# Chunk attention two heads at a time, on alternating halves of the TensorE array

## The chip, the cores and the metric

The kernel runs on one core of a Trainium2 chip. The metric is the device time of one execution in microseconds: the median of 3 runs is 1926.85 us.

## What is computed

A two-layer streaming encoder over 512 frames of width 1024, in float32: an S5 and gated-DeltaNet mixer, memory cross-attention and a SwiGLU FFN in the first layer; chunk attention, cross-attention and FFN in the second. The change touches chunk attention alone (16 heads of 64, chunks of 64 frames, each attending to its own chunk and the 8 before it, which is here all that went before):

```python
q = rms_norm(qkv[:, :, 0], q_g); k = rms_norm(qkv[:, :, 1], k_g); v = qkv[:, :, 2]
def one_chunk(c):
    ...
    s = jnp.einsum('bqhd,bkhd->bhqk', q_c, k_c) * scale + bias
    s = jnp.where((band_pos + start) >= 0, s, -1e30)
    p = jax.nn.softmax(s, axis=-1)
    return jnp.einsum('bhqk,bkhd->bqhd', p, v_c)
```

## The kernel before, in words

Each engine has its own instruction stream, written out by hand; semaphores (`wait_ge`, `then_inc`) tie them together, and the order of a stream is the order of the calls in it. `ca_pe`, `ca_act`, `ca_dve` and `ca_sp` are the parts of chunk attention on TensorE, ScalarE, VectorE and the SP queue.

Queries and keys stand transposed in SBUF, `cqT` and `ckT`: head h occupies partitions 64*(h % 2) to 64*(h % 2)+63 of plane h // 2, so a product of them uses half of the array's rows. The 512 queries of a head are four blocks i of 128; block i sees the keys 0 to 128*(i+1), so its scores are 128*(i+1) wide. One head goes through:

- scores, TensorE (`ca_scores_pe`, L1761): four products into PSUM banks 0 to 3. A float32 product of this kind stands in the trace as two passes, each with its own weight load.
- sums, VectorE (`ca_dve.sums`, L1838 to L1848): a mask of 64x64 on the bias, then `tensor_tensor_reduce` (L1844) adds the bias, writes the block to SBUF (`p_c`) and takes each row's maximum. In the trace this is CUSTOM_DVE_ANT_0 with a read-out of the accumulator.
- exponentials, ScalarE (`ca_act.exps`, L1821), in place, with row sums.
- rescale, VectorE (L1859, L1862): reciprocal, then four multiplies in place.
- transposes, TensorE (`ca_turn_p_pe`, L1771): ten blocks of 128x128, in four groups s of 4, 3, 2 and 1 into PSUM banks 4 to 6 in turn.
- copies (`ca_copy`): group s goes to SBUF (`pT_c`), 0 and 3 by ScalarE (L1793), 1 and 2 by VectorE (L1795).
- values, TensorE (`ca_values_pe`, L1780): four products of 128 rows with 64 columns of weights, into partitions 0 to 63 or 64 to 127 of bank 7.
- output, in two parts that sum to float32: ScalarE copies bank 7 to `c_oT[0]` (L1831), rounded; VectorE subtracts that from bank 7 into `c_oT[1]` (L1853, `out_lo`).

TensorE's order is transposes of h, scores of h+2, values of h. `p_c` and `pT_c` have two sets each. The bias of each head comes by a DMA on SP's queue into a ring of four. GpSimd has nothing to do in this stage. After it the output projection begins (`split_outproj_pe`, L308 to L310). Before it, query and key rows are transposed (`ca_turn_pe`, L1734).

Three other places are spoken of: `piece_lo` (L280), VectorE's subtraction for a 2048-column weight piece; the FFN's loops (L1627 on VectorE, L1637 and L1639 on GpSimd); and the states of the S5 mixer (L787), whose matmuls write partitions 0 to 63 and 64 to 127 of PSUM by turns:

```python
for g in range(S5_G):
    gp, g2 = g // 2, g % 2
    ins = pe.matmul(ps[g2 * 64:g2 * 64 + 64, 4 + 2 * ri + gp // 8, ...],
                    WT[:, g, ri * 64:ri * 64 + 64], U2[:, g, :], start=True, stop=True)
```

Of the kernel before, what the change touches and what calls it, by code (L numbers as in the profile page):

```python
# [44 lines left out]
BAND_W = SEQ  # L45
BAND_E = BAND_W + P - 1

# [22 lines left out]
def build_program(nc, A):  # L70
    ctx = ExitStack()
    with ctx:
# [9 lines left out]
        with nc.sbuf_tensor("params", [P, N_PAR], F32) as par:  # L82
# [21 lines left out]
                   "cat_hi": ("go_sq", TT), "cat_lo": ("go_n", TT), "mem_kept": ("cat_s5", 1),  # L104
                   "s5_pad": ("conv", 12), "y_v": ("conv", 20), "y_a": ("u_s", 4)}
# [975 lines left out]
        LEVELS = 5  # L1081

# [592 lines left out]
        c_max, c_neg, c_sum, c_rec = cs(2, TT), cs(2, TT), cs(2, TT), cs(2, TT)  # L1675
        ck_rows = rows(high_b)
        cqT, ckT = feat(high_c), feat(high_d)
        p_c = [reg(arena + 2048 * n, TT, SEQ) for n in range(2)]
        pT_c = [reg(at_b + 2048 * n, TT, SEQ) for n in range(2)]
# [72 lines left out]
        def ca_scores_pe(pe, h):  # L1752
            r = slice(64 * (h % 2), 64 * (h % 2) + 64)
            if h == 0:
# [8 lines left out]
        def ca_turn_p_pe(pe, h):  # L1763
            for s in range(TT):
                m = 4 * h + s
                if m >= 3:
                    pe.wait_ge(sem(COPY[(m - 3) % 4][0]), 2 * ((m - 3) // 4) + COPY[(m - 3) % 4][1])
                for i in range(s, TT):
                    if s == 0:
                        pe.wait_ge(sem("c_p"), 4 * h + i + 1)  # L1770
                    ins = pe.transpose(ps[:, 4 + m % 3, i * P:(i + 1) * P], p_c[h % 2][:, i, s * P:(s + 1) * P], ident)  # L1771
                ins.then_inc(sem("c_tr"), 1)

        def ca_values_pe(pe, h):
            r = slice(64 * (h % 2), 64 * (h % 2) + 64)
            if h > 0:
                pe.wait_ge(sem("c_ol"), h)
            for s in range(TT):
                pe.wait_ge(sem(COPY[s][0]), 2 * h + COPY[s][1])
                ins = pe.matmul(ps[r, 7, s * P:SEQ], v_rows[:, s, h * CD:(h + 1) * CD], pT_c[h % 2][:, s, s * P:SEQ],  # L1780
# [421 lines left out]
```

## Time and profile before

| | |
|---|---|
| median of 3 runs | 1926.85 us (1925.38 to 1929.81) |
| span of the profiled execution, first to last instruction | 1924.5 us |
| busy: TensorE, VectorE, ScalarE, GpSimd | 93%, 42%, 33%, 12% of the span |
| mean granted TensorE clock | 0.963 of 2.4 GHz |
| instructions | 20683 |

The profile gives the profiled execution's span and no time of its own outside it; the runs are other executions. In the profile PE is TensorE's matmul, PEld its weight load, DVE VectorE, ACT ScalarE, POOL GpSimd, SP the queue that issues DMAs. A busy PE is not PE at its peak: matmuls are pipelined, and a record ends later than the next begins. L12 is line 12 of the kernel. A row names output<-input, with partitions x elements; `sb` is the large SBUF tensor in which most tiles of this stage lie, and `h_hi` and `h_lo` there are the output's two parts. For matmuls rows*columns of the array come first.

### The profile page before, as it was taken

To read this page: it belongs to the slowest core of one execution; us is meant where nothing else is said; L and a number is where in the kernel's file an instruction comes from. 1 tells how busy PE (TensorE), PEld (TensorE's weight loads), DVE (VectorE), ACT (ScalarE), POOL (GpSimd) and SP (SyncE) were. 2 spreads that over 40 slices of the span, in tenths; PEclk is the share of its full clock that TensorE was granted. 3 is DMA by queue.
4 is the path that set the end of the run, shared out by engine and by line. 5 is a ranking of instruction groups with operands and counts; after the bars stand their busy time and mean duration, and the time that the engine had idled before them with its cause. 6 is when DMAs were issued, how large, how long until landed. Compare 5 with 4: busy or idle time off the path is not lost.

```text
span 1924.5 us, 20683 instructions
## 1 busy us (share of the span) xinstructions
PE 1781.8 (93%) x8392; PEld 1434.0 (75%) x8392; DVE 811.5 (42%) x1054; ACT 629.4 (33%) x998; POOL 238.5 (12%) x285
## 2 busy tenths in 40 slices
PE   6997676999998999999998999999998999999998
PEld 5877656977775788888787887557785778888787
DVE  4744554445534433333214344673535243333212
ACT  5222053224433332232113233563434232232210
POOL 1783003230000011111000000000000011111000
PEclk9997587999999999999999999999999999999999
DMA  5215001012520223332322231121430223433321
GB/s 195 88 41 92 0 1 45 3 65 88 175 66 22 80 73 88 107 88 87 107 90 88 88 109 50 39 67 63 157 109 22 66 66 89 107 87 87 103 94 66
DMA packets 146796, 151.97 MB, mean 79 GB/s; under 512 B 8865, under 2 KB 109345, under 8 KB 146593
## 3 DMA queue, kind: packets, MB, share of 16 engines
q1 hardware_dynamic: 146720, 150.92, 26.1%
q8 instruction: 53, 0.87, 0.2%
q14 instruction: 23, 0.18, 0.0%
HBM read 147.76 MB, written 3.15 MB: 78 GB/s over the span
## 4 chain that ended last, share of the span: by engine, by line
PE 85%; DVE 9%; ACT 3%; issue 2%; DMA 0%; POOL 0%; SPq 0%; DVEq 0%; ACTq 0%
PE ps L308 22%; PE ps L310 22%; PE ps L309 22%; PE ps L1761 2%; PE ps L1780 2%; PE ps L1479 2%; PE ps L1502 2%; PE ps L382 1%; PE ps L1119 1%; PE ps L1129 1%; PE ps L893 1%; PE ps L1134 1%; DVE sb L346 1%; PE ps L834 1%; PE ps L736 1%
## 5 line engine op out<-in xcount | busy, mean ns | idle before, releaser
L308 PE MATMUL ps<-h_hi,w_hi 128*128 128x512 f32 x864 | 339.9, 393 | 2.1 <-DVE w_lo_ab L280 2.1
L309 PE MATMUL ps<-h_lo,w_hi 128*128 128x512 f32 x864 | 341.3, 395 | 0.0
L280 DVE TENSOR_TENSOR w_lo<-raw,w_hi 128x2048 fp32r<-128x2048 f32 x70 | 160.5, 2292 | 411.3 <-ACT w_hi L276 411.3
L276 ACT ACTIVATE w_hi<-raw 128x2048 fp32r<-128x2048 f32 x84 | 160.7, 1914 | 437.3 <-PE ps L310 435.8
L310 PE MATMUL ps<-h_hi,w_lo 128*128 128x512 f32 x704 | 279.7, 397 | 0.0
L308 PE MATMUL ps<-w_hi,h_hi 128*128 128x512 f32 x512 | 201.8, 394 | 6.6 <-DVE h_lo L1555 2.8
L310 PE MATMUL ps<-w_hi,h_lo 128*128 128x512 f32 x512 | 200.2, 391 | 0.0
L309 PE MATMUL ps<-w_lo,h_hi 128*128 128x512 f32 x512 | 198.7, 388 | 0.0
L308 PEld LDWEIGHTS ps<-h_hi,w_hi 128*128 128x128 f32 x864 | 162.4, 188 | 41.2 <-DVE w_lo_ab L280 2.6
L309 PEld LDWEIGHTS ps<-h_lo,w_hi 128*128 128x128 f32 x864 | 162.2, 188 | 41.1
L1637 POOL CAST a_hi<-up 128x512 f32 x44 | 26.9, 610 | 1229.6 <-DVE up L1625 1229.6
L1627 DVE TENSOR_TENSOR w_lo<-raw,w_hi 128x2048 fp32r<-128x2048 f32 x44 | 140.7, 3198 | 52.0 <-ACT w_hi L1613 52.0
L310 PEld LDWEIGHTS ps<-h_hi,w_lo 128*128 128x128 f32 x704 | 132.1, 188 | 30.9
L1613 ACT ACTIVATE w_hi<-raw 128x2048 fp32r<-128x2048 f32 x44 | 84.2, 1914 | 204.3 <-PE ps L310 204.3
L1625 DVE TENSOR_TENSOR up<-up,ps 128x512 f32<-128x512 f32 x44 | 30.3, 688 | 276.6 <-PE ps L310 276.6
L308 PE MATMUL ps<-w_hi,a_hi 128*128 128x512 f32 x352 | 138.5, 394 | 1.8 <-DVE up L1625 1.8
L310 PE MATMUL ps<-w_hi,a_lo 128*128 128x512 f32 x352 | 137.6, 391 | 0.0
L309 PE MATMUL ps<-w_lo,a_hi 128*128 128x512 f32 x352 | 136.6, 388 | 0.0
L308 PEld LDWEIGHTS ps<-w_hi,h_hi 128*128 128x128 f32 x512 | 96.2, 188 | 28.7 <-DVE h_lo L1555 4.5
L310 PEld LDWEIGHTS ps<-w_hi,h_lo 128*128 128x128 f32 x512 | 95.8, 187 | 22.5
L309 PEld LDWEIGHTS ps<-w_lo,h_hi 128*128 128x128 f32 x512 | 96.1, 188 | 20.8
L308 PEld LDWEIGHTS ps<-w_hi,a_hi 128*128 128x128 f32 x352 | 66.2, 188 | 16.2 <-DVE up L1625 2.7
(331 smaller groups left out, 2546.7 us busy)
## 6 DMA issues: line engine op xcount, KB each, us to landing
raw<-in_f_w_gate SPq DMA_DIRECT2D x44, 512.0 KB, 4.0
raw<-in_f_w_up SPq DMA_DIRECT2D x44, 512.0 KB, 5.3
raw<-in_f_w_down SPq DMA_DIRECT2D x44, 512.0 KB, 4.2
raw<-in_xa_w_kv SPq DMA_DIRECT2D x16, 1024.0 KB, 5.0
raw<-in_c_w_qkv SPq DMA_DIRECT2D x12, 1024.0 KB, 5.1
raw<-in_ab_w_in SPq DMA_DIRECT2D x10, 1024.0 KB, 5.5
raw<-in_xa_w_q SPq DMA_DIRECT2D x8, 1024.0 KB, 5.0
raw<-in_xa_w_out SPq DMA_DIRECT2D x8, 1024.0 KB, 5.0
```

The source lines that it names most:

```text
L276: a.activation(w_hi[:, n % 2, :], raw[n % 2], ACT.Copy).then_inc(sem("w_hi"), 1)
L280: v.tensor_tensor(w_lo(n)[:, n % 2, :], raw[n % 2], w_hi[:, n % 2, :].bitcast(F32), ALU.subtract).then_inc(sem("w_lo"), 1)
L308: pe.matmul(out, a[0], b[0], start=start, stop=False)
L309: pe.matmul(out, a[0], b[1], start=False, stop=False)
L310: return pe.matmul(out, a[1], b[0], start=False, stop=stop)
L1479: ins = pe.matmul(ps[:, 2 * (h % 2) + i // 2, (i % 2) * 256:(i % 2) * 256 + 256], qT[:, 2 * h + d, i * P:(i + 1) * P], xk_T[:, 2 * h + d, ...
L1502: ins = pe.matmul(ps[:, 6 + d, :], xv[:, s, h * XD + d * P:h * XD + (d + 1) * P], pT_x[h % 2][:, s, :], start=(s == 0), stop=(s == 1))
L1613: a.activation(w_hi[:, slot, :], raw[slot], ACT.Copy).then_inc(sem("w_hi"), 1)
L1625: v.tensor_tensor(prod[:, s, :], gsil[:, s, :], ps[:, 4 * s + 1, :], ALU.mult).then_inc(sem(f"f{l}_free"), 1)
L1627: v.tensor_tensor(w_lo(n0)[:, slot, :], raw[slot], w_hi[:, slot, :].bitcast(F32), ALU.subtract).then_inc(sem("w_lo"), 1)
L1761: pe.matmul(ps[:, i, 0:n], cqT[r, h // 2, i * P:(i + 1) * P], ckT[r, h // 2, 0:n], start=True, stop=True).then_inc(sem("c_s"), 1)
L1780: ins = pe.matmul(ps[r, 7, s * P:SEQ], v_rows[:, s, h * CD:(h + 1) * CD], pT_c[h % 2][:, s, s * P:SEQ], start=(s == 0), stop=(s == TT - 1) ...
```

## The change

Heads go through the stage in pairs m, heads 2m and 2m+1 as e = 0 and 1.

- Scores and values are issued for e = 0 and e = 1 by turns. The scores' operands lie on partitions 0 to 63 and 64 to 127, so they use the two halves of the array's rows; the values write the two halves of its columns.
- The scores of a pair take banks 0 to 3 (`ca_score`): blocks of 512 and 256 wide of head e in bank e, 384 and 128 wide in bank 2+e. The order is 512, 384, 128, 256 (`CA_ROWS`), and the 256-wide ones wait until VectorE has summed both 512-wide ones.
- There is one set of `pT_c` for each e, and two sets of `p_c` for each; both are stored without the empty half.
- ScalarE's exponentials of pair m+1 and its copies of pair m alternate; the first exponential stands before the first copy. Copies 0, 2, 5 and 7 of the eight are ScalarE's, 1, 3, 4 and 6 VectorE's (`COPY`).
- VectorE rescales three of the four blocks; GpSimd multiplies the 512-wide one by the broadcast reciprocal (`ca_pool`) and sets the masks on the bias.
- Output copy and low part are made once a pair, on 128 partitions.

```diff
-        def ca_scores_pe(pe, h):
-            r = slice(64 * (h % 2), 64 * (h % 2) + 64)
...
-            for i in range(TT):
-                if h > 0:
-                    pe.wait_ge(sem("c_s2"), 4 * (h - 1) + i + 1)
-                n = (i + 1) * P
-                pe.matmul(ps[:, i, 0:n], cqT[r, h // 2, i * P:(i + 1) * P], ckT[r, h // 2, 0:n], start=True, stop=True).then_inc(sem("c_s"), 1)
+        def ca_scores_pe(pe, m):
...
+                pe.wait_ge(sem("c_s2"), 8 * m)
+            for n, i in enumerate(CA_ROWS):
+                if n == 3:
+                    pe.wait_ge(sem("c_s2"), 8 * m + 2)
+                for e in range(2):
+                    r = slice(64 * e, 64 * e + 64)
+                    ins = pe.matmul(ca_score(i, e), cqT[r, m, i * P:(i + 1) * P], ckT[r, m, 0:(i + 1) * P], start=True, stop=True)
+                ins.then_inc(sem("c_s"), 1)
...
+        def ca_turn_p_pe(pe, m):
+            for n in range(8):
+                s, e = n // 2, n % 2
+                g = 8 * m + n
+                if g >= 3:
+                    pe.wait_ge(sem(COPY[(g - 3) % 8][0]), 4 * ((g - 3) // 8) + COPY[(g - 3) % 8][1])
+                for i in range(s, TT):
+                    if s == 0:
+                        pe.wait_ge(sem(RESCALE[i][0]), after(RESCALE[i][0], RESCALE[i][1] * (2 * m + e) + RESCALE[i][2]))
+                    ins = pe.transpose(ps[:, 4 + g % 3, i * P:(i + 1) * P], p_c(m, e, i)[:, s * P:(s + 1) * P], ident)
+                ins.then_inc(sem("c_tr"), 1)
...
+            for s in range(TT):
+                for e in range(2):
+                    pe.wait_ge(sem(COPY[2 * s + e][0]), 4 * m + COPY[2 * s + e][1])
+                    h = 2 * m + e
+                    ins = pe.matmul(ps[64 * e:64 * e + 64, 7, s * P:SEQ], v_rows[:, s, h * CD:(h + 1) * CD], pT_c(e, s),
+                                    start=(s == 0), stop=(s == TT - 1), skip_group_check=True)
...
-            for h in range(CH):
-                ca_turn_p_pe(pe, h)
-                if h + 2 < CH:
-                    ca_scores_pe(pe, h + 2)
-                ca_values_pe(pe, h)
+            for m in range(CH // 2):
+                ca_turn_p_pe(pe, m)
+                if m + 2 < CH // 2:
+                    ca_scores_pe(pe, m + 2)
+                ca_values_pe(pe, m)
...
+            for m in range(CH // 2):
+                if m + 1 < CH // 2:
+                    a.wait_ge(sem("c_max"), m + 2)
+                for e in range(2):
+                    for j in range(4):
+                        if m + 1 < CH // 2:
+                            exp(m + 1, e, CA_EXP[j])
+                        n = 4 * e + j
+                        if COPY[n][0] == "c_pa":
+                            ca_copy(a, m, n)
+                a.wait_ge(sem("c_o"), m + 1)
+                a.activation(c_oT[0][:, m, :].rearrange("p (i n) -> p i n", i=TT),
+                                  ps[:, 7, :].rearrange("p (i n) -> p i n", i=TT)[:, :, ::-1], ACT.Copy).then_inc(sem("c_oc"), 1)
...
+            for m in range(CH // 2):
+                if m > 0:
+                    out_lo(m - 1)
+                for n in range(8):
+                    if COPY[n][0] == "c_pv":
+                        ca_copy(v, m, n)
+                    if n == 4 and m + 1 < CH // 2:
+                        rescale(m + 1, 0)
+                if m + 2 < CH // 2:
+                    sums(m + 2)
+                if m + 1 < CH // 2:
+                    rescale(m + 1, 1)
+            out_lo(CH // 2 - 1)
+
+        def ca_pool(g):
...
+            for m in range(CH // 2):
+                g.wait_ge(sem("c_mask"), after("c_mask", min(2 * m + 4, CH)))
+                for e in range(2):
+                    g.wait_ge(sem("c_rec"), after("c_rec", 2 * m + e + 1))
+                    p = p_c(m, e, TT - 1)
+                    g.tensor_tensor(p, p, bc(c_rec[:, m % 2, e, TT - 1], 1, SEQ), ALU.mult).then_inc(sem("c_pg"), 1)
```

The changed file's lines are some 16 to 27 further down: L1777 are its scores, L1789 its transposes, L1799 its values, L1815 ScalarE's copies, L1841 its exponentials, L1858 its output copy. (`ca_turn_p_pe` and the loops of ScalarE and VectorE did the same for single heads before; they are printed above.)

TensorE's stream in the steady part of the stage. Before, one head of transposes, scores and values, and the next head's transposes:

```order
L1771 MATMUL ps<-sb 128x128 x10
L1761 MATMUL ps<-sb 128x128
L1761 MATMUL ps<-sb 128x256
L1761 MATMUL ps<-sb 128x384
L1761 MATMUL ps<-sb 128x512
L1780 MATMUL ps<-sb 64x512
L1780 MATMUL ps<-sb 64x384
L1780 MATMUL ps<-sb 64x256
L1780 MATMUL ps<-sb 64x128
```

With the change, one pair:

```order
L1789 MATMUL ps<-sb 128x128 x20
L1777 MATMUL ps<-sb 128x512 x2
L1777 MATMUL ps<-sb 128x384 x2
L1777 MATMUL ps<-sb 128x128 x2
L1777 MATMUL ps<-sb 128x256 x2
L1799 MATMUL ps<-sb 64x512 x2
L1799 MATMUL ps<-sb 64x384 x2
L1799 MATMUL ps<-sb 64x256 x2
L1799 MATMUL ps<-sb 64x128 x2
```

Each kind of matmul stands twice in a row, once for each half, and the score blocks come in another order.

ScalarE's stream at the same place. Before, from one head's output copy (L1831) to the next, with copies of transposed blocks (L1793) and exponentials (L1821):

```order
L1831 ACTIVATE h_hi<-ps 64x512
L1793 ACTIVATE sb<-ps 128x512
L1793 ACTIVATE sb<-ps 128x128
L1821 ACTIVATE sb<-sb 128x128
L1821 ACTIVATE sb<-sb 128x256
L1821 ACTIVATE sb<-sb 128x384
L1821 ACTIVATE sb<-sb 128x512
```

With the change, from one pair's output copy (L1858) on, with copies (L1815) and exponentials (L1841):

```order
L1858 ACTIVATE h_hi<-ps 128x512
L1841 ACTIVATE sb<-sb 128x512
L1815 ACTIVATE sb<-ps 128x512
L1841 ACTIVATE sb<-sb 128x384
L1841 ACTIVATE sb<-sb 128x256
L1815 ACTIVATE sb<-ps 128x384
L1841 ACTIVATE sb<-sb 128x128
L1841 ACTIVATE sb<-sb 128x512
L1841 ACTIVATE sb<-sb 128x384
L1815 ACTIVATE sb<-ps 128x256
L1841 ACTIVATE sb<-sb 128x256
L1841 ACTIVATE sb<-sb 128x128
```

Both copies stood ahead of the exponentials before; now the widest exponential of the next pair is ahead of the first copy, and two more are ahead of the second.

## Rows read from the trace of the kernel before

**Rows 1.** Busy time by stretch: from:to, us of the stretch, then each engine's busy time and instructions, granted clock, DMA

```profile
1240.00:1270.00 30.00, 29.37 (x124) 16.08 (x125) 23.36 (x86) 17.27 (x54) 0.00 (x0) 1.00 0.20 45
```

**Rows 2.** Chain of waits, two heads: start us, length us, what

```profile
1245.92 0.33 PE ps L1771
1246.25 2.35 PE ps L1761 x8
1248.60 2.30 PE ps L1780 x8
...
1257.21 0.57 issue
...
1257.80 0.61 ACT sb L1793
...
1258.45 0.33 PE ps L1771
```

**Rows 3.** Timeline and chain at the stage's start and end: start us, length us, what

```profile
1194.42 2.29 DVE L280 TENSOR_TENSOR w_lo<-raw,w_hi 128x2048 fp32r<-128x2048 f32 x1 [1.33 <-ACT w_hi L276]
...
1202.69 2.74 PE ps L1771 x10
...
1305.50 0.50 PE L308 MATMUL ps<-w_hi,h_hi 128*128 128x512 f32 x1 [1.41 <-DVE h_lo L1853]
```

**Rows 4.** Timeline of weight loads, values of one head: start, length, what

```profile
1249.01 0.14 PEld L1780 LDWEIGHTS ps<-sb 128*64 128x64 f32 x1 [0.29 <-issue]
1249.44 0.14 PEld L1780 LDWEIGHTS ps<-sb 128*64 128x64 f32 x1 [0.29 <-issue]
```

**Rows 5.** Timeline of TensorE, alternating column halves in the S5 stage

```profile
178.77 3.95 PE L787 MATMUL ps<-sb 128*64 128x64 f32 x128 [1.18 <-ACT memT L970]
```

**Rows 6.** Timeline of VectorE, one head

```profile
1242.70 1.27 DVE L1862 TENSOR_SCALAR sb<-sb 128x128 f32<-128x128 f32 x4
1244.04 0.11 DVE L1838 MEMSET sb<- 64x64 f32 x1
...
1245.23 0.69 DVE L1844 CUSTOM_DVE_ANT_0 sb<-ps,sb 128x512 f32<-128x512 f32 x1
1245.84 0.08 DVE L1844 DVE_READ_ACCUMULATOR2_ANT sb<- 128x1 f32 x1
...
1246.16 0.69 DVE L1853 TENSOR_TENSOR h_lo<-ps,h_hi 64x512 fp32r<-64x512 f32 x1
```

**Rows 7.** Timeline of ScalarE, one head's exponentials

```profile
1247.33 0.60 ACT L1821 ACTIVATE sb<-sb 128x384 f32<-128x384 f32 x1
...
1247.93 0.71 ACT L1821 ACTIVATE sb<-sb 128x512 f32<-128x512 f32 x1
1248.54 0.19 ACT L1821 ACTIVATION_READ_ACCUMULATOR sb<-sb 128x1 f32 x1
```

**Rows 8.** Timeline of TensorE, query and key transposes before the stage

```profile
1185.16 7.04 PE L1734 MATMUL ps<-sb 128*128 128x128 f32 x63
```

**Rows 9.** Groups by line and shape, GpSimd, whole span

```profile
L1097 POOL TENSOR_TENSOR sb<-sb 128x512 f32<-128x512 f32 x20 | 24.8, 1275 | 18.0 <-PE ps L1119 17.9
```

**Rows 10.** Timelines of GpSimd and VectorE, in the first FFN and in the input projection

```profile
921.69 1.29 POOL L1639 TENSOR_TENSOR a_lo<-up,a_hi 128x512 f32 x1 [0.16 <-POOL a_hi L1637]
...
921.95 3.18 DVE L1627 TENSOR_TENSOR w_lo<-raw,w_hi 128x2048 fp32r<-128x2048 f32 x1 [1.20 <-ACT w_hi L1613]
...
60.44 2.29 DVE L280 TENSOR_TENSOR w_lo_ab<-raw,w_hi 128x2048 fp32r<-128x2048 f32 x1 [2.62 <-ACT w_hi L276]
...
60.54 2.34 POOL L579 TENSOR_TENSOR sb<-sb 128x48 f32<-128x48 f32 x1
```

**Rows 11.** Busy time by stretch, as in rows 1, before and where the clock fell

```profile
1184.00:1191.00 7.00, 7.00 (x60) 6.73 (x59) 4.16 (x6) 4.61 (x7) 0.00 (x0) 1.00 0.01 2
...
1195.00:1198.30 3.30, 1.65 (x7) 0.78 (x6) 3.20 (x9) 0.69 (x1) 0.00 (x0) 1.00 0.00 0
1198.30:1212.00 13.70, 12.30 (x26) 5.68 (x25) 8.35 (x35) 5.34 (x18) 0.00 (x0) 0.50 0.15 39
```

More of the change, by code:

```diff
@@ L1763, in ca_turn_p_pe @@
[L1763 to L1767, printed above, removed]
+            else:
+                pe.wait_ge(sem("c_s2"), 8 * m)
[6 more added lines that the diff above has]
+                ins.then_inc(sem("c_s"), 1)
@@ new lines, in ca_dve, with sums, out_lo, rescale @@
+        def ca_dve(v):
+            def sums(m):
+                v.wait_ge(sem("c_mask"), after("c_mask", 2 * m + 2))
+                if m >= 2:
+                    v.wait_ge(sem("c_tr"), 8 * (m - 1))
+                for n, i in enumerate(CA_ROWS):
+                    v.wait_ge(sem("c_s"), 4 * m + (1, 3, 3, 4)[n])
+                    for e in range(2):
+                        v.tensor_tensor_reduce(out=p_c(m, e, i), in0=ca_score(i, e),
+                                                    in1=bias_ring[:, (2 * m + e) % 4, BAND_W - (i + 1) * P:BAND_W], scale=1.0, scalar=-3.0e38,
+                                                    op0=ALU.add, op1=ALU.max, accum_out=c_max[:, m % 2, e, i:i + 1]).then_inc(sem("c_s2"), 1)
+                v.wait_ge(sem("c_s2"), 8 * m + 8)
+                v.tensor_scalar(c_neg[:, m % 2], c_max[:, m % 2], -1.0, None, ALU.mult).then_inc(sem("c_max"), 1)
+            def out_lo(m):
+                v.wait_ge(sem("c_oc"), m + 1)
+                v.tensor_tensor(c_oT[1][:, m, :].rearrange("p (i n) -> p i n", i=TT),
+                                ps[:, 7, :].rearrange("p (i n) -> p i n", i=TT)[:, :, ::-1],
+                                c_oT[0][:, m, :].bitcast(F32).rearrange("p (i n) -> p i n", i=TT), ALU.subtract).then_inc(sem("c_ol"), 1)
+            def rescale(m, e):
+                v.wait_ge(sem("c_exp"), 8 * m + 4 * e + 4)
+                v.reciprocal(c_rec[:, m % 2, e], c_sum[:, m % 2, e]).then_inc(sem("c_rec"), 1)
+                v.wait_ge(sem("c_rec"), after("c_rec", 2 * m + e + 1))
+                for i in (2, 1, 0):
+                    p = p_c(m, e, i)
+                    v.tensor_scalar(p, p, c_rec[:, m % 2, e, i:i + 1], None, ALU.mult).then_inc(sem("c_pv2"), 1)
@@ L1864, in ca_dve @@
             sums(0)
             sums(1)
-            rescale(0)
-            for h in range(CH):
-                if h > 0:
-                    out_lo(h - 1)
-                ca_copy(v, h, 1)
-                ca_copy(v, h, 2)
-                if h + 1 < CH:
-                    rescale(h + 1)
-                if h + 2 < CH:
-                    sums(h + 2)
-            out_lo(CH - 1)
+            rescale(0, 0)
+            rescale(0, 1)
+            for m in range(CH // 2):
+                if m > 0:
+                    out_lo(m - 1)
[8 more added lines that the diff above has]
+                    rescale(m + 1, 1)
```

111 lines of the change are left out of this document (47 added, 64 removed).

## Prediction

> **What bounds the kernel now.** I read the page first: TensorE is busy 93% of the span, and 85% of the chain that ended last is TensorE. Then the stage that the change touches, chunk attention, some 112 us long and the only stage whose instructions change. In it VectorE is busy 78% and ScalarE 58% of a steady stretch [rows 1]. The chain of waits through one head [rows 2] says what sets its pace: 2.35 us of scores (L1761), 2.30 us of values (L1780), some 1.2 us in which ScalarE's output copy (0.57 us, shown as "issue") and its first copy of transposed probabilities (0.61 us, L1793) follow each other, and a last 0.33 us of transposes (L1771). The same piece stands at 1245.92 and at 1258.45, two heads on: 12.53 us a pair, 6.27 us a head. So nearly three quarters of a head's pace are the two products on half of the array, and the rest is a hand-over between TensorE and ScalarE. The first head's transposes begin at 1202.69, after a start in which VectorE is held until 1196.71 by a weight piece (1194.42 and 2.29 us), and the output projection begins at 1305.50 [rows 3].
>
> **Can two halves run together?** A half-array matmul takes two passes. In the two of 512 columns the weights load 0.43 us apart [rows 4]: 0.84 ns a column and pass. All passes of one head, 2 x 1280 columns, are 2.15 us, which is what the chain shows. In the older S5 stage, alternate matmuls go to the two column halves: 128 passes of 64 columns start within 3.73 us (3.95 less the last one's 0.22), 29 ns each, 0.455 ns a column [rows 5]. That is 1.84 times the rate of the half-array matmuls of the stage [rows 4], so **column halves do overlap** in float32, moving data and all. No row of this trace shows alternate row halves. Between full overlap and none I take overlap, since columns are the nearest row, and keep the other end as a rival. Starts stay in order, and a product has two passes on its own half, so the overlap has an edge: pass A1 alone, A2 beside B1, B2 beside the next A1.
>
> **The change part by part, as one loop.** With halves together no engine is full. VectorE per pair: eight sums, two reciprocals, six multiplies, four copies and one 128-partition low part, about 8.2 us by the kinds of [rows 6]; ScalarE about 6.9 us; TensorE 20 x 0.11 us of transposes and some 5.5 us of products. The pace is then set by the chain that closes on itself. Its links for one pair:
> - ScalarE, 3.57 us: output copy 0.50 (0.59 long, of which the next overlaps some 0.10, as copies and exponentials do), the exponential of the widest block 0.83 (1247.93 to the end of its read-out at 1248.73, and a gap of 0.03, since a copy with two waits starts only when ScalarE has drained, as the whole 0.57 us of "issue" before the copy shows), copy of 512 0.49 (0.61 long), exponential of 384 0.60, of 256 0.62 (0.49 by width, drained again), copy of 384 0.53 by width [rows 2, 7]. The order rows of the change show this queue: the exponentials of the next pair now stand **ahead of and between** the copies, and the first of them behind the output copy.
> - TensorE, 0.58 us: the last four transposes, each 7.04/63 = 0.11 us [rows 8], and a switch between kinds of matmul of 0.15 us (between 2.30-2.15 and 2.35-2.15 us [rows 2]).
> - TensorE to VectorE, 1.50 us: the two 512-wide scores, three slots of 0.43 us, and 0.21 us until VectorE may read (a pass of 64 columns lasts 0.22 us [rows 5] and streams for 0.05; with a hand-over of 0.04).
> - VectorE, 1.34 us: two sums of 512, 0.61 us until the next may start, the second with its read-out and hand-over 0.73 [rows 6].
> - TensorE, 0.85 us: the 256-wide scores, which now wait for those sums because they reuse the bank: three slots of 0.215 us and a switch of 0.2 us. The values of the pair are queued behind them, and ScalarE's output copy behind the values.
> - TensorE, 2.79 us: the values, 0.43 us and then 2 x (0.43+0.32+0.22+0.11), and 0.21 us until ScalarE reads.
> Sum 10.63 us a pair against 12.53.
>
> **GpSimd's multiply.** It takes two SBUF operands, 1275 ns [rows 9], and replaces some 0.4 of the 1.27 us of VectorE's four multiplies [rows 6]. In the same moment VectorE multiplies the three narrower blocks in SBUF. The two engines exclude each other [rows 10]: VectorE's subtraction of 2048 columns, 2.29 us alone, takes 3.18 us when it starts 0.26 us into GpSimd's 1.29 us, and a GpSimd product of only 48 columns takes 2.34 us when VectorE's is under way, longer than one of 512. Both have two SBUF operands; VectorE's multiply here has one and a scalar, so the trace leaves open whether it is held. Not held, or held in VectorE's favour, it costs nothing in the loop: GpSimd ends the first head's block some 4 us before TensorE wants it, and the second head's with 1.4 us to spare before ScalarE copies the transposes behind it. Held in GpSimd's favour, VectorE's copy and the sums behind it come 1.27 us later, less 0.5 us that they wait for scores anyway: 0.8 us a pair. The ends are 0 and 0.8; I take 0.4, the middle, as the nearest rows show exclusion but not for this form: 11.0 us a pair. SBUF — State Buffer of the Trainium skill, section "SBUF: two separate sides", says that a VectorE operation in a two-port mode holds the shared ports for its whole length, and so would hold this multiply too; by it the loop is 11.4 us and the time 2 us longer. For operations with two operands the trace agrees [rows 10].
>
> **Edit by edit, the rest.** Sixteen masks of 0.11 us [rows 6] leave VectorE for GpSimd, which is idle and does them a pair ahead: nothing. Output copies and low parts go from 16 on 64 partitions to 8 on 128, the low part 0.69 us at 64 partitions [rows 6] and, as its width sets it, at 128: they are in the sums above. Bias loads stay 16, on SP's queue behind the same weight pieces; each waits for a pair that is two pairs back, over 10 us ahead of need: nothing. The single set of transposed blocks (two before) waits for the values of the pair before, which are on TensorE ahead of the transposes anyway: nothing. If that cover went, it would be one copy, 0.6 us a pair.
>
> **The start and the end.** Both first pairs must be summed before the first multiply. From 1196.75: sums of pair 0, 3.45 us and 0.4 us of waiting for its last scores, to 1200.6; scores of pair 1 at the half clock that the trace shows from 1198.3 to 1212 [rows 11], 2.8 us for the widest two; its sums, which are by then bound by the scores, end near 1207.2; reciprocal and multiplies to 1208.5. That is 5.8 us **later** than now. The first pair takes 12.2 us, 1.2 more than the next, as part of it is still at half clock; five pairs at 11.0; the seventh 7.2 us (10.63 less the three links of scores, and a switch); the eighth 8.1 us (transposes and copies by turns 3.7, values with a switch 3.0, output copy 0.64, low part and hand-over 0.77). 1208.5+12.2+55.0+7.2+8.1 = 1291.0. I add 1.2 us, half of the 2.5 that one more stretch of half clock would cost. The stage ends at 1292.2 instead of 1305.50: **13.3 us less**. What follows is the same work, and moves with it. The profiled execution's span is 1924.5 us, 2.35 below the median of three runs, 1926.85; the difference goes on the median: 1913.5 us.
>
> **Rivals.**
> - Row halves don't overlap, columns do. For it: no row shows them. The widest scores then take a fourth slot (+0.42), the 256-wide one too (+0.21) and wait for the other blocks' passes (+0.2): 11.5 to 11.9 us a pair, the start 3 us later. 1919 us.
> - No overlap at all, so the change does not do what it says. Against it: the S5 stage [rows 5]. Values then take 4.3 us (+1.73), with the above 13.2 us a pair, more than now, because the waits on ScalarE and VectorE are new and nothing pays for them. Stage end 1308 to 1312: 1931 us, slower.
> - The clock. TensorE's granted clock went from 2.4 to 1.2 GHz at 1198.3, after 3.30 us with 1.65 us of TensorE work [rows 11]. In the new loop about 4.2 us pass between values and scores with nothing but 20 transposes, 2.2 us of work, twice in 22 us; so a fall in each pair can be. Against it: the average is 7.6 us of work in 11, and 63 transposes alone, back to back for 7.04 us, ran at full clock [rows 8, 11]. The loop's five TensorE terms hold 4.96 us of passes, which double. It decides the sign once the half clock covers over 0.55 of the loop: 11.0+0.55 x 4.96 = 13.7 us a pair gives back all. At 0.6 with the edges it is some 5 us more than now: 1932 us. TensorE: Matmul & The Clock Gate of the Trainium skill, section "Part 4: PE-mode transpose", has it that transposes don't count as work for the clock, which speaks for this rival; the rows where they held the full clock don't bear that out [rows 8, 11].
> - A further wait that I haven't seen (GpSimd's block for the second head, which starts only after all eight sums, is the nearest, should it come later than its 1.4 us to spare) adds 1.2 to 1.7 us a pair. 1924 us, no change.
>
> **How the numbers follow.** Main case 0.64, row halves 0.12, no overlap 0.05, clock 0.09, further wait 0.10. A measurement of this kernel can tell 0.2% from no change, 3.9 us. Faster: 0.64+0.12+0.01 = 0.77; same 0.09, the rest of the further wait; slower 0.05+0.09 = 0.14. The main case alone spans 1908 to 1918: below, GpSimd free (-2), no added half clock (-1.2) and copies that don't drain ScalarE (-2); above, the 0.8 us a pair and all of the half clock. The range goes from 1907 to 1925, up to row halves and most of the further wait; it leaves out about 0.17.
>
> **What would show it.** Right: pairs of score passes that start 0.21 us apart on average; one pair every 10.6 to 11.4 us; ScalarE's output copy released by values, and the copies by nothing; first transposes near 1208 to 1210; VectorE idle some 2 to 3 us a pair. GpSimd's price is read off VectorE's three multiplies: 0.9 us together, or 1.3 us more. Wrong: score passes 0.43 us apart, a granted clock under 0.95 between 1220 and 1280, or a pair that takes over 12.5 us.

## The result and the profile after

| | before | changed |
|---|---|---|
| median of 4 runs each | 1928.24 us (1925.38 to 1929.81) | 1907.90 us (1906.81 to 1909.53) |
| ratio | | 0.9894, 95% interval 0.9881 to 0.9906 |
| span of the profiled execution | 1924.5 us | 1907.7 us |

Faster by 20.3 us. The time lies inside the range and 5.6 us under the number given; the gain forecast was 13.3 us. (Of the 7.0 us between the two gains 1.4 are the median before, which is 1928.24 us with a fourth run and was 1926.85 with three.)

Busy time by stretch, first the same one as in [rows 1], then two of the start at half clock and all of the steady part, and last one long before the stage:

```profile
1240.00:1270.00 30.00, 23.67 (x156) 13.65 (x156) 28.63 (x91) 18.52 (x63) 7.66 (x12) 1.00 0.33 106
...
1201.90:1208.70 6.80, 5.46 (x20) 2.37 (x16) 4.39 (x24) 4.47 (x16) 0.00 (x0) 0.50 0.25 78
...
1212.15:1218.98 6.83, 5.63 (x22) 4.06 (x22) 4.91 (x11) 5.16 (x18) 2.19 (x4) 0.50 0.09 31
1218.98:1275.00 56.02, 44.24 (x294) 25.12 (x290) 53.17 (x171) 31.97 (x107) 13.80 (x21) 1.00 0.25 76
...
116.50:119.90 3.40, 3.35 (x8) 2.68 (x9) 2.25 (x1) 0.90 (x2) 3.09 (x5) 0.50 0.00 0
```

TensorE, 29.37 of 30 us busy before, now has 23.67; VectorE has gone from 23.36 to 28.63. The clock fell twice in the start and never in the steady part. The last row tells how to compare the two traces: this execution had 3.40 us of half clock at 116.5 us, in work that the change does not touch and that ran at full clock in the trace before, and it reaches the stage later. So times are compared from the end of VectorE's weight piece, 1196.71 in [rows 3] and 1200.31 here (a shift of 3.60 us):

```profile
1198.02 2.29 DVE L283 TENSOR_TENSOR w_lo<-raw,w_hi 128x2048 fp32r<-128x2048 f32 x1 [1.33 <-ACT w_hi L279]
...
1211.68 0.71 PE L1789 MATMUL ps<-sb 128*128 128x128 f32 x4 [3.20 <-DVE sb L1887]
...
1288.87 0.50 PE L311 MATMUL ps<-w_hi,h_hi 128*128 128x512 f32 x1 [1.42 <-DVE h_lo L1877]
```

The first transposes are at 1208.08 on the clock of the trace before (1202.69 there), the output projection at 1285.27 (1305.50 there): the stage ends 20.2 us earlier, which is the whole difference of the medians. From the end of the weight piece to the output projection it takes 88.6 us, 108.8 before; this length is "the stage" below.

The chain of waits through one pair, from output copy to output copy, the counterpart of [rows 2]:

```profile
1244.01 0.03 ACT h_hi L1858
...
1247.67 0.19 DVE sb L1883
...
1247.92 0.30 issue
1248.22 0.91 DVE sb L1887
...
1249.75 1.23 DVE sb L1869 x4
...
1251.02 0.70 PE ps L1777 x4
1251.72 2.33 PE ps L1799 x16
...
1254.07 0.03 ACT h_hi L1858
```

10.06 us a pair, where the prediction had 11.0. ScalarE, the sums, the 256-wide scores and the values stand in it as forecast. The transposes and the two widest scores do not: in their place the chain goes through VectorE's reciprocal (L1883) and its multiplies (L1887), of which the second, 256 wide, takes 0.91 us until the next may start. So the loop that closes here is not the one forecast. VectorE was to be idle 2 to 3 us a pair; with 28.63 of 30 us busy it is idle under 0.5.

Timeline of weight loads, score passes of a pair and values of a pair, the counterpart of [rows 4]:

```profile
1248.43 0.19 PEld L1777 LDWEIGHTS ps<-sb 64*128 64x128 f32 x2 [0.23 <-issue]
1248.86 0.84 PEld L1777 LDWEIGHTS ps<-sb 64*128 64x128 f32 x6 [0.23 <-issue]
...
1252.13 0.14 PEld L1799 LDWEIGHTS ps<-sb 128*64 128x64 f32 x2 [0.29 <-issue]
1252.56 0.14 PEld L1799 LDWEIGHTS ps<-sb 128*64 128x64 f32 x2 [0.29 <-issue]
```

Loads now come **in twos**, one for each half: the two values' loads together take 0.14 us, as long as one did, and the twos are 0.43 us apart at 512 columns, as single loads were. The scores' do the same. Rows and columns both overlap fully; no pass runs alone at the edge.

VectorE's and GpSimd's timelines, the two places where both multiply:

```profile
1243.29 1.79 DVE L1887 TENSOR_SCALAR sb<-sb 128x384 f32<-128x384 f32 x3
...
1247.88 1.66 DVE L1887 TENSOR_SCALAR sb<-sb 128x384 f32<-128x384 f32 x3
```

```profile
1243.33 1.04 POOL L1920 TENSOR_TENSOR sb<-sb 128x512 f32<-128x512 f32 x1 [4.19 <-DVE sb L1883]
...
1247.99 1.21 POOL L1920 TENSOR_TENSOR sb<-sb 128x512 f32<-128x512 f32 x1 [3.26 <-DVE sb L1883]
```

Three multiplies of 384, 256 and 128 columns take 1.66 and 1.79 us, where all four took 1.27 us before [rows 6]. The multiplies by line and shape, first those of the second head (1243.25 to 1243.35), then those of the first (1248.15 to 1248.30):

```profile
L1887 DVE TENSOR_SCALAR sb<-sb 128x384 f32<-128x384 f32 x1 | 1.3, 1299 | 0.0
...
L1887 DVE TENSOR_SCALAR sb<-sb 128x256 f32<-128x256 f32 x1 | 1.1, 1130 | 0.0
L1887 DVE TENSOR_SCALAR sb<-sb 128x384 f32<-128x384 f32 x1 | 0.4, 420 | 0.0
```

One multiply of three is stretched each time: the first, 1299 ns where it takes 420 for the other head, or the second.

### The profile page after: what moved, and what is told of

It is laid out like the page before. It is cut to its first block, busy times and chain, and to the rows that moved or that the text cites. A ratio compares the mean times of both kernels' runs of the same rounds, so it can differ in the third digit from the quotient of the medians.

```text
span 1907.7 us, 20656 instructions
## 1 busy us (share of the span) xinstructions
PE 1749.7 (92%) x8392; PEld 1420.5 (74%) x8392; DVE 809.2 (42%) x1006; ACT 622.0 (33%) x990; POOL 259.2 (14%) x317
## 4 chain that ended last, share of the span: by engine, by line
PE 84%; DVE 10%; ACT 3%; issue 2%; DMA 0%; POOL 0%; SPq 0%; DVEq 0%; ACTq 0%
PE ps L311 22%; PE ps L313 22%; PE ps L312 22%; PE ps L1480 2%; PE ps L1503 2%; PE ps L385 1%; PE ps L1120 1%; PE ps L1130 1%; PE ps L1799 1%; PE ps L896 1%; PE ps L1135 1%; PE ps L739 1%; DVE sb L349 1%; PE ps L837 1%; PE ps L838 1%
```

## Experiments

After the result three theories stood. **H**: the pace is the loop of the prediction, with the halves wholly side by side, and GpSimd's multiply lengthens it by holding VectorE's. **P** and **V**, for what the halves are worth: each half's overlap is paid in full (P), or VectorE, full by now, hides most of it (V). The ratios below are to the runs of the kernel before on the same chip; "a pair" is from output copy to output copy in the steady part. The stage is read from one profiled execution of each run, the median from all of them. Outside the stage all runs do the same work, yet the profiled executions spend between 1813 and 1819 us there; so where median and stage disagree by some 3 us, that difference is not shown to come from the edit.

| run | edit | median us | ratio, 95% interval | stage us | us a pair |
|---|---|---|---|---|---|
| changed | | 1907.90 | 0.9894 (0.9881 to 0.9906) | 88.6 | 10.06 |
| pool_after | GpSimd's multiply waits for VectorE's | 1902.26 | 0.9868 (0.9846 to 0.9889) | 86.1 | 9.62 |
| pool_none | VectorE does all four | 1902.50 | 0.9862 (0.9843 to 0.9880) | 83.6 | 9.67 |
| rows_seq | scores one head after the other | 1909.11 | 0.9897 (0.9878 to 0.9915) | 93.0 | 10.57 |
| cols_seq | values one head after the other | 1916.32 | 0.9933 (0.9913 to 0.9953) | 99.9 | 11.61 |
| rows_apart | the same for scores, with a wait | 1935.41 | 1.0044 (1.0030 to 1.0059) | 116.6 | 12.40 (14.0 to 15.1 with half clock) |
| cols_apart | the same for values, with a wait | 1924.66 | 0.9988 (0.9978 to 0.9997) | 106.4 | 12.47 |
| apart | both with waits | 1947.66 | 1.0102 (1.0085 to 1.0119) | 132.4 | 14.81 (16.5 with half clock) |
| expfirst | first exponential moved up | 1905.52 | 0.9883 (0.9867 to 0.9900) | 86.9 | 9.84 |
| mix_expfirst | that, and GpSimd only once a pair | 1899.24 | 0.9848 (0.9831 to 0.9864) | 80.1 | 9.01 |
| gp_before | kernel before with GpSimd's multiply | 1932.64 | 1.0025 (1.0015 to 1.0035) | 114.1 | 6.48 a head |

### What GpSimd's multiply costs

pool_after adds one wait to `ca_pool`:

```diff
                     g.wait_ge(sem("c_rec"), after("c_rec", 2 * m + e + 1))
+                    g.wait_ge(sem("c_pv2"), after("c_pv2", 3 * (2 * m + e) + 3))
```

> GpSimd starts its multiply of a head only when VectorE has ended its three of that head; all else is the changed kernel (1907.9 us). Theory H: the multiplies of VectorE are held by GpSimd's (1299 and 1130 ns where 0.41 and 0.35 would do, 1.67 us a pair), and this hold is on the loop that sets the pace of 10.06 us. Then VectorE's three multiplies fall from about 1.8 to 0.9 us, the pair to between 8.4 and 9.3 us, and the time by 6 to 12 us, to 1896 to 1902 us. Theory F: the loop through ScalarE and TensorE would fill the gap with another wait (ScalarE's exponentials are late anyway): the multiplies get shorter, the time stays within 2 us of 1907.9.

pool_none takes the multiply away from GpSimd:

```diff
-                for i in (2, 1, 0):
+                for i in (2, 1, 0, 3):
...
-                    g.tensor_tensor(p, p, bc(c_rec[:, m % 2, e, TT - 1], 1, SEQ), ALU.mult).then_inc(sem("c_pg"), 1)
```

> VectorE multiplies all four blocks, the 512-wide one last; GpSimd keeps the masks alone. Theory H: 1.67 us of hold go and two multiplies of some 0.4 us come, so a pair takes about 0.9 us less than 10.06 and the time falls by 5 to 8 us, to 1900 to 1903 us: the part of the change that moved the widest block to GpSimd costs more than it saves. Theory F, VectorE's work is hidden: within 2 us of 1907.9. If GpSimd's help is worth what the change's idea says, it is slower by 3 to 6 us.

Both medians fell by some 5.5 us, which is the edge of H's range for pool_after and inside it for pool_none. The paces were not H's: 9.62 and 9.67 us a pair, where it had 8.4 to 9.3 and about 9.2. F was wrong on the time, but had the reason: with the hold gone, another wait fills part of the gap. In the traces the stage of pool_after is 2.5 us shorter than the changed kernel's, and 2.2 of it are five pairs; the other 3 us of its median lie outside the stage and are not shown to come from the edit. Of pool_none's 5.0 us five pairs are 1.9, and 1.5 lie in the first pair, where the clock's second fall lasted 3.4 us and not 6.8. Letting GpSimd wait and not using it at all give the same pace. In pool_after, VectorE's three multiplies (L1887) and GpSimd's (L1921) of one head:

```profile
1242.41 0.88 DVE L1887 TENSOR_SCALAR sb<-sb 128x384 f32<-128x384 f32 x3
...
1243.74 0.69 DVE L1869 CUSTOM_DVE_ANT_0 sb<-ps,sb 128x512 f32<-128x512 f32 x1 [0.25 <-PE ps L1777]
```

```profile
1243.46 1.04 POOL L1921 TENSOR_TENSOR sb<-sb 128x512 f32<-128x512 f32 x1 [3.29 <-DVE sb L1887]
```

The three take 0.88 us when GpSimd is idle, against 1.66 and 1.79: GpSimd's multiply holds them for 0.78 and 0.91 us, 1.7 us a pair. It holds nothing else that can be seen: a sum of 512 under way beside it takes 0.69 us, as it does alone. And the chain of pool_after is the prediction's loop, link for link:

```profile
1241.84 0.66 PE ps L1789 x4
1242.49 1.08 PE ps L1777 x4
...
1243.74 1.32 DVE sb L1869 x4
...
1245.11 0.70 PE ps L1777 x4
1245.81 2.33 PE ps L1799 x16
...
1248.16 0.03 ACT h_hi L1858
...
1251.46 0.55 PE ps L1789 x3
```

From transposes to transposes 9.62 us a pair. So the hold costs the loop 10.06 - 9.62 = 0.44 us a pair, though VectorE loses 1.7: only the first head's hold, 0.78 us, stands ahead of the sums, and 0.34 us of that they would have waited for the scores anyway; behind the second head's there is spare time.

gp_before gives the kernel before that one part of the change:

```diff
+                v.reciprocal(c_rec[:, h % 2, :], c_sum[:, h % 2, :]).then_inc(sem("c_rec"), 1)
-                for i in range(TT):
+                for i in range(TT - 1):
...
+            for h in range(CH):
+                g.wait_ge(sem("c_rec"), after("c_rec", h + 1))
+                g.tensor_tensor(p_c[h % 2][:, 3, :], p_c[h % 2][:, 3, :], bc(c_rec[:, h % 2, 3], 1, SEQ), ALU.mult).then_inc(sem("c_pg"), 1)
```

> The kernel before, one head at a time, with one part of the change alone: GpSimd multiplies the 512-wide block of each head at the same time as VectorE its three. Theory H (GpSimd holds VectorE's multiplies, and it costs time only where VectorE has none to spare): VectorE is idle 1.4 us of the 6.27 us of a head there, and loses some 0.9 us of stall less the 0.4 us of the multiply it no longer does; the transposes of a head wait for GpSimd's 1.28 us instead of VectorE's 1.27 us. So within 3 us of the kernel before: 1925 to 1931. Rival G (every delay of the first transposes and of the sums is paid): 16 heads by 0.5 us, 8 us slower, 1936. Rival F (VectorE's 0.4 us are a gain): 16 x 0.4 = 6 us faster, 1922.

4.2 us slower, over H's bound of 3 and under G's 8. VectorE's idle time of 1.4 us a head was not all there to be used. VectorE's row, and the chain of one head:

```profile
1245.03 1.76 DVE L1863 TENSOR_SCALAR sb<-sb 128x128 f32<-128x128 f32 x3
```

```profile
1251.29 0.19 DVE sb L1859
...
1252.59 0.67 DVE sb L1863 x2
...
1253.48 1.74 DVE sb L1844 x8
...
1255.45 2.30 ACT sb L1821 x8
...
1257.77 0.19 DVE sb L1859
```

The three multiplies take 1.76 us where four took 1.27 [rows 6]. Reciprocal, multiplies, sums of the next head, their exponentials and the next reciprocal form a loop of their own: 6.48 us with the hold, so about 6.0 without the 0.49 us, under the 6.27 us of the kernel before. The slack was some 0.3 us, not 1.4, since VectorE idles in that loop while ScalarE is at its exponentials.

### What the halves are worth

rows_seq and cols_seq only put the products in another order, the first head's before the second's:

```diff
-            for n, i in enumerate(CA_ROWS):
-                if n == 3:
+            for e, i in [(e, i) for e in range(2) for i in CA_ROWS[:3]] + [(0, 1), (1, 1)]:
+                if (e, i) == (0, 1):
```

> The scores of the two heads are no longer issued by turns: 512, 384 and 128 wide of the first head, then of the second, then the two 256-wide ones. Same products, same banks. Theory P (both row halves run wholly side by side, pass beside pass, and scores stand on the loop): the 512-wide scores of the second head come 1.7 us later, of which some 0.7 are hidden by VectorE's own lateness, and the 256-wide ones stay side by side: 0.8 to 1.2 us a pair, 6 to 10 us more, 1914 to 1918 us; passes of one head stand 0.43 us apart. Theory V (VectorE is the bound, at 96% busy, and the row halves bring next to nothing): within 3 us of 1907.9.

```diff
-            for s in range(TT):
-                for e in range(2):
+            for e in range(2):
+                for s in range(TT):
```

> The values of the two heads are no longer issued by turns, but all four of the first head, then of the second. Theory P: the values of a pair take 4.3 us instead of 2.15 and stand on the loop with all their length, so a pair takes 2.1 us more and the time rises by 14 to 17 us, to 1922 to 1925 us. Theory V: VectorE is the bound and covers most of it, under 6 us more.

Scores in a row cost 1.2 us, values in a row 8.4, both far less than P had. By the stage they cost some 4.5 and 11.3 us. The medians read like V for the scores, and lie between V and P for the values; but the traces show that the edit didn't do what it was for. The three widest scores of both heads in rows_seq, and, by line and shape, what TensorE was running between 1238.30 and 1238.50:

```profile
1237.07 2.96 PE L1776 MATMUL ps<-sb 64*128 64x512 f32 x12
```

```profile
L1776 PE MATMUL ps<-sb 64*128 64x384 f32 x2 | 0.8, 482 | 0.0
L1776 PE MATMUL ps<-sb 64*128 64x512 f32 x1 | 0.7, 693 | 0.0
```

In the program the first head's 512, 384 and 128 come before the second head's 512. In the trace the second head's 512 is running beside the first head's 384: **TensorE started a pass of the free half ahead of its turn**. The first two 512 passes ran alone, then the halves overlapped again. In cols_seq it was the same: the second head's first pass of values started at 1244.06, beside the first head's first 256-wide pass, with three passes of the first head still to come, and the values took 3.88 us on the chain. Every pair comes from the same calls, so an order fixed in the instruction stream would repeat. In the seventh pair of cols_seq it does not: the first head's second 256-wide pass went first too, and the second head's 512 started only at 1287.09; at 1287.00:

```profile
L1799 PE MATMUL ps<-sb 128*64 128x256 f32 x2 | 0.6, 379 | 0.0
```

In rows_seq the pair took 10.57 us, which is pool_after's 9.62 and the 0.96 us by which its scores (2.04 us on the chain instead of 1.08) were longer. Against the changed kernel only 0.51 us shows, since GpSimd's hold of 0.44 us then lies beside the scores.

So the halves had to be kept apart by waits: TensorE signals the end of the first head's products to itself and waits for that before the second's.

```diff
+            for part, blocks in enumerate((CA_ROWS[:3], CA_ROWS[3:])):
...
                 for e in range(2):
+                    for i in blocks:
...
+                    if e == 0:
+                        ins.then_inc(sem("c_scale"), 1)
+                        count["apart"] = count.get("apart", 1) + 1
+                        pe.wait_ge(sem("c_scale"), count["apart"])
```

cols_apart has the same wait between the values of the two heads, apart has both edits.

> The changed kernel with the score products alone kept apart: TensorE waits until the first head's three widest scores are done before it starts the second head's, and again for the 256-wide ones; values by turns as in the changed kernel. It prices the row halves' overlap by itself, which putting the scores in a row did not, since TensorE then started passes of the second head ahead of their turn. Theory H (the loop with its measured links): the second head's 512-wide scores end some 1.6 us later (1.71 us of the first head's three blocks and 0.04, then 0.86, against 1.08), of which 0.6 us was the first head's sum that ran meanwhile and 0.5 us VectorE's stall by GpSimd, which no longer lies on the way; the 256-wide ones take 0.7 us more: 11.0 to 12.0 us a pair, 1915 to 1923 us. Rival V (row halves are worth next to nothing, as the run with scores in a row, 1909.1 us, said): 1908 to 1911 us.

> The changed kernel with the value products alone kept apart: TensorE waits until the first head's values are done before the second head's; scores by turns as in the changed kernel. It prices the column halves' overlap by itself. Theory H (values are wholly on the chain that closes on itself): 4.7 us instead of 2.33 us of values; 2.37 us a pair less what VectorE's stall of some 0.4 us had hidden: 12.0 to 12.4 us a pair, 8 pairs by 1.9 to 2.4 us, 15 to 19 us more: 1923 to 1927 us. Rival V (VectorE is 96% busy and its queue hides a good part): 8 to 11 us more, as in the run with values in a row: 1916 to 1919 us. Together with the run that keeps only scores apart: where both are short of the run with everything apart (14.8 us a pair at full clock, 1947.7 us) by over 5 us, the rest is the clock, which fell there three times in the loop.

> The changed kernel with no two halves at work together: TensorE waits until the first head's scores (and its values) are done before it starts the second head's. Same instructions, other order and three waits a pair (before the second head's three widest scores, before its 256-wide one, before its values). This gives the price of the rival in which halves do not overlap, that the prediction put at 13.2 us a pair and 1931 us, slower than before. Theory H (measured links, where two scores orders in a row cost little because VectorE was late): the values take 4.3 + 0.3 us of waiting instead of 2.33, scores 256 wide 0.86 + 0.2 instead of 0.70, the two widest and what lies between them 2.15 + 0.3 + 0.9 us instead of 1.08: 10.06 + 2.3 + 0.4 + 0.5 to 2.0 = 13.3 to 14.8 us a pair, 1930 to 1940 us. Rival S (the gain comes mostly from ScalarE and VectorE working on two heads at once, not from the array's halves): under 12.5 us a pair and faster than the kernel before, under 1924 us.

Chain of rows_apart, its scores in a pair at full clock (widest three of each head, then the 256-wide ones), and busy time of the stretch before one fall of its clock:

```profile
1266.31 1.93 PE ps L1778 x6
...
1268.28 1.14 PE ps L1778 x2
...
1270.95 0.71 PE ps L1778 x2
...
1271.70 0.70 PE ps L1778 x2
```

```profile
1253.20:1256.60 3.40, 2.69 (x8) 1.34 (x8) 2.10 (x7) 0.30 (x3) 0.00 (x0) 0.99 0.00 0
```

And the values in the chain of cols_apart:

```profile
1244.20 2.31 PE ps L1799 x8
...
1246.55 2.38 PE ps L1799 x8
```

At full clock the prices add up. Scores apart: 1.93 + 0.04 + 1.14 - 1.08 = 2.03 us for the three widest and 0.71 + 0.04 + 0.70 - 0.70 = 0.75 for the 256-wide ones, and 9.62 + 2.78 = 12.40. Values apart: 4.73 - 2.33 = 2.40, and 10.06 + 2.40 = 12.46 (12.47). Both: 9.62 + 2.78 + 2.40 = 14.80 (14.81). P was right in substance: each half's overlap is on the path. But the prices include what the waits cost by themselves, since the second head then starts only when the first head's last pass has ended. The passes of one head's three widest scores follow each other in 2 x (0.43+0.32+0.11) = 1.72 us, and the wait made that 1.97; for the 256-wide ones it made 0.43 into 0.75, and for the values 2.16 into 2.35. Without that, each overlap is worth an estimated 2.2 us a pair, rows as much as columns. For rows even that holds only while both sums wait for one signal, as in this edit (below).

cols_apart came out where H had it (1923 to 1927). rows_apart ran 12 us over H's upper end, for two reasons. The smaller lies in the edit: sums of both heads wait for one signal, given after the second head's block, so the first head's sum, 0.6 us, could not run meanwhile, as the expectation had it; with a signal of its own the rows' price would be lower by up to that. No run tried it. The larger is the clock. It was at half from 1201.9 to 1222.4, and again at 1229.3 (before the first output copy), 1242.9, 1256.6 and 1283.9 for 3.4 to 6.8 us each; the three of five pairs in which it fell took 14.0 to 15.1 us. Of the 27.5 us over the changed kernel, 9.3 lie in the start, 11.7 are five pairs by 2.34 us at full clock, and some 7 the falls among those pairs. In the 3.40 us before the fall at 1256.6 TensorE worked 2.69 us, all of it passes of 64 rows, one at a time. The same passes in the pair behind, 2.67 us of the 3.40 from 1269.6 on, were followed by no fall. cols_apart, as long a pair, kept the full clock throughout its steady part. What makes the difference stays open. apart shows the same: 14.81 us a pair, as H had it, but falls at 1256.2, 1273.3 and 1304.0 as well as a longer half clock in the start, and so 8 us over H's upper end.

### A better version

In the changed kernel ScalarE waits for the values with a full exponential still to do. expfirst moves it ahead of the output copy:

```diff
+                if m + 2 < CH // 2:
+                    a.wait_ge(sem("c_max"), m + 3)
+                    exp(m + 2, 0, CA_EXP[0])
                 a.wait_ge(sem("c_o"), m + 1)
                 a.activation(c_oT[0][:, m, :].rearrange("p (i n) -> p i n", i=TT),
```

mix_expfirst has that too, and in it GpSimd multiplies the first head's block only, after VectorE's three; VectorE does the second head's four:

```diff
-                for i in (2, 1, 0):
+                for i in (2, 1, 0) + ((3,) if e else ()):
...
+                g.wait_ge(sem("c_pv2"), after("c_pv2", 7 * m + 3))
+                p = p_c(m, 0, TT - 1)
```

> The changed kernel with one thing moved: ScalarE computes the first exponential of the pair after next before this pair's output copy instead of behind it; GpSimd multiplies as in the changed kernel. Theory H (in the changed kernel GpSimd's multiplies have filled VectorE to 96%, 9.63 of 10.06 us a pair, so VectorE is all but the bound): of the 0.83 us taken out of ScalarE's part of the chain at most 0.4 us a pair come back, 0 to 3 us: 1905 to 1908. Rival C (the chain over ScalarE sets the pace and VectorE's fullness is only its shadow): 0.83 us a pair over 7 pairs, 5.8 us, comes back: 1902.

> GpSimd multiplies only the first head's widest block, after VectorE's three multiplies; VectorE does all four of the second head; and ScalarE computes the first exponential of the pair after next before this pair's output copy, while TensorE is still on the values. Theory H (the loop is the chain of the prediction with the halves fully side by side, and GpSimd's multiply costs VectorE only when they run together): against the kernel whose GpSimd waits, 1902.3 us and 9.62 us a pair, the exponential of 0.83 us leaves the chain; VectorE, 37.93 of 45 us busy there, that is 8.1 us a pair, plus 0.45 us for the fourth multiply of one head, becomes the next bound at about 8.6 us, so 8.8 to 9.2 us a pair and 7 pairs x 0.4 to 0.8 us less: 1896 to 1900 us. Rival C (ScalarE is the bound, since the moved exponential only changes its place in a full queue): its busy time of 6.4 us a pair speaks against it, but then the pair stays at 9.6 us and the time at 1902.

Both times lie in H's ranges. expfirst takes 0.83 us out of ScalarE's part and gets 0.22 back: between 1240 and 1262 us its chain has no piece of ScalarE at all, and 77% of it is VectorE's, 29% the multiplies (L1890). With the hold gone too, a pair takes 9.01 us, 0.61 under pool_after; that is the move and the other split of the multiplies together. Busy time in mix_expfirst:

```profile
1220.00:1265.00 45.00, 39.20 (x262) 22.70 (x261) 41.66 (x156) 32.07 (x106) 6.12 (x13) 1.00 0.28 91
```

VectorE is at 93%, TensorE at 87%. VectorE is not the bound that H expected: between 1240 and 1262 us 62% of the chain is TensorE's, and no multiply stands in it. **1899.24 us**, 8.7 us under the changed kernel and 1.5% under the one before. GpSimd's part of it was not run without the moved exponential, so what each of the two edits brings is not told apart.

## Why the prediction was right, and where its sum was off

The forecast of a faster kernel and its mechanism, two halves at work together, held. Two terms of the sum were too large, and the loop was the forecast one only with GpSimd's multiply out of the way.

**What bounds, and the direction**: right. The stage's pace was two half-array products one after the other; side by side they no longer set it.

**Halves overlap**: right, for columns from [rows 5] and for rows, which no row had shown. "Starts stay in order, so the overlap has an edge: pass A1 alone" was **the step that failed**. Passes of both halves start together, as the loads in twos show: the second head's first pass starts 7 ns behind the first head's first (1247.902 and 1247.895), ahead of its second (1248.429). The three slots of scores (0.43 us too many), of 256-wide scores (0.215) and the values' extra 0.43 were 1.07 us of the 10.63.

**The loop, link by link**, against pool_after, where nothing else is in it:

| link | forecast us | measured us |
|---|---|---|
| ScalarE | 3.57 | 3.31 |
| transposes and switch | 0.58 | 0.66 |
| widest scores, hand-over | 1.50 | 1.25 |
| sums | 1.34 | 1.36 |
| 256-wide scores | 0.85 | 0.70 |
| values | 2.79 | 2.35 |
| sum | 10.63 | 9.63 |

TensorE's three products came 0.84 us shorter: 1.07 for the edge, less what switches and hand-overs took more. ScalarE came 0.26 us shorter. There the second mis-sized step is "a copy with two waits starts only when ScalarE has drained". It need not. ScalarE's timeline in the changed kernel, each copy (L1815) with the read-out ahead of it:

```profile
1245.12 0.19 ACT L1841 ACTIVATION_READ_ACCUMULATOR sb<-sb 128x1 f32 x1
1245.21 0.59 ACT L1815 ACTIVATE sb<-ps 128x512 f32<-128x512 f32 x1
...
1246.69 0.19 ACT L1841 ACTIVATION_READ_ACCUMULATOR sb<-sb 128x1 f32 x1
1246.78 0.48 ACT L1815 ACTIVATE sb<-ps 128x384 f32<-128x384 f32 x1
```

Both copies start 0.09 us behind the start of a read-out that lasts 0.19. What the 0.57 us of "issue" in [rows 2] were is left open; copies behind an exponential don't share it.

**GpSimd**: 0.4 us a pair taken, between 0 and 0.8; 0.44 measured. But the middle was no knowledge, and that it fits is luck. What was left open is now shown: VectorE's multiply with one operand and a scalar is held, for 0.78 and 0.91 us. In the changed kernel VectorE's first multiply starts 0.11 us before GpSimd's for one head, and then only its second is held, and GpSimd's own lasts 1.21 us instead of 1.04; for the other head it starts 0.04 us before, and is held itself. A sum that reads PSUM is not held. SBUF — State Buffer of the Trainium skill, section "SBUF: two separate sides", has a lock on shared ports that whoever starts first keeps for its whole instruction; these runs agree as to what is held, and on who wins down to those 0.04 us of recorded starts, where it was the other. The 0.8 us that the prediction took for GpSimd always winning were 1.27 us of hold ahead of the sums, less 0.5 of waiting for scores; measured are 0.78 less 0.34.

**Start and end**: first transposes 1208.08 by the clock of the trace before, forecast 1208.5. From there to the first output copy 12.21 us (12.2), five pairs at 10.06 instead of 11.0 (-4.7), the seventh 6.76 (7.2), the eighth to the last low part 7.87 (8.1), and the added 1.2 us of half clock did not come: of the two falls in the start one lies before the first transposes, the other inside the 12.2. Together 0.4 + 4.7 + 0.4 + 0.2 + 1.2 = 6.9 us, the difference between 13.3 and 20.2.

**Rivals.** No overlap was priced at 13.2 us a pair and 1931 us. Kept apart by waits, it is 14.8 and 1947.7: slower than before, as said, and by more, because the waits of this edit stood in the chain as well and the clock fell with them. The 2.3 us a pair over the 12.53 of before are what going by pairs costs when the halves do not overlap; some 0.8 of them are the waits' own. Row halves alone were priced at 11.5 to 11.9 and 1919; kept apart they gave 12.4 and 1935.4, slower than before. The clock rival did not happen in the changed kernel, 1.00 over 56 us, but it is real: rows_apart showed it, with pairs of 15.1 us. It rested on the stretch between values and scores with nothing but 20 transposes, and that stretch did not bring the clock down: from 1218.98 on it held 1.00. TensorE: Matmul & The Clock Gate of the Trainium skill, section "Part 4: PE-mode transpose", has it that transposes don't count for the clock; by it the rival was likelier than it proved here.

## What to carry to other kernels

When work on a small tile is limited by matmuls that use half of the array, issue two of them for opposite halves next to each other: in these runs a pair took 2.8 us more with row halves kept apart by waits and 2.4 us more with column halves, of which the overlap itself is an estimated 2.2 us each. Without the overlap the pairing was a loss. Then look for the loop that closes through the other engines and read each link from the trace; idle time of an engine is only slack if it does not lie inside such a loop (1.4 us idle, 0.3 us of slack). Moving an elementwise operation to an idle GpSimd can cost more than it saves: put it where VectorE works from PSUM, or leave it. Here even that brought nothing that could be measured, 9.62 us a pair against 9.67 without GpSimd. And compare variants by the stage that the edit touches: single executions differed by up to 6 us in work that no edit had touched.

## What the hardware did that was not expected

- TensorE ran a pass of the free half ahead of program order: the second head's 512-wide pass ran beside the first head's 384-wide one in rows_seq. In the steady pairs of both rows_seq and cols_seq it went ahead of three passes of the other half, not more. To keep halves apart, only a semaphore served.
- GpSimd's SBUF multiply of 512 columns holds VectorE's SBUF multiply for 0.78 to 0.91 us, even when the latter's record starts 0.04 us earlier, but not its first when that starts 0.11 us earlier; it leaves a sum with one PSUM operand at 0.69 us.
- Alone, GpSimd's 512-wide multiply took 1.04 us here; [rows 9] has 1.275 us as the mean for an operation of that kind in another stage.
- The clock fell three times among the steady pairs with row halves kept apart and never with column halves kept apart, though a pair at full clock is as long in both, 12.4 and 12.5 us.
